# Early score tiles over three buffers, held gates two quads at a time, one-hot rows from GpSimd and ScalarE

## What is computed

```python
def peer_ffn(h, w_q, sub_keys, expert_u, expert_v):     # 8 heads, 128 x 128 experts, top 16
    q = (hb @ w_q).reshape(n, PEER_HEADS, 2, PEER_HALF_2)
    s = jnp.einsum('nhcd,hckd->nhck', q, sub_keys)
    sc, ix = lax.top_k(s, PEER_TOPK)
    cand = sc[:, :, 0, :, None] + sc[:, :, 1, None, :]
    cidx = ix[:, :, 0, :, None] * PEER_N_KEYS + ix[:, :, 1, None, :]
    top, pos = lax.top_k(cand.reshape(n, PEER_HEADS, PEER_TOPK * PEER_TOPK), PEER_TOPK)
    eidx = jnp.take_along_axis(cidx.reshape(n, PEER_HEADS, -1), pos, axis=-1)
    gate = jax.nn.softmax(top, axis=-1)
    act = jax.nn.gelu(jnp.einsum('nhed,nd->nhe', expert_u[eidx], hb), approximate=False)
    return jnp.einsum('nhe,nhed->nd', (gate * act).astype(hb.dtype), expert_v[eidx])
```

## Time and profile before

| | us |
|---|---|
| runs | 4035.78, 4033.04, 4031.42 (median 4033.04) |
| profiled execution | 4032.07, span on the core 4030.0, mean granted TensorE clock 0.918 |

### The profile page before, as it was taken

One profiled execution on the slowest core, in us unless ns is written; L12 is line 12 of the kernel. 1 busy time (PEld: TensorE's weight loads), 2 busy tenths in 40 slices (PEclk: granted clock), 3 DMA queues, 4 the chain that ended last, 5 costly groups with the idle time before them and its releaser, 6 DMA issues. The chain is left out here.

```text
span 4030.0 us, 59683 instructions
## 1 busy us (share of the span) xinstructions
PE 3481.5 (86%) x20736; PEld 3011.1 (75%) x20736; DVE 2486.0 (62%) x5005; ACT 1510.8 (37%) x2312; POOL 427.0 (11%) x460
## 2 busy tenths in 40 slices
PE   6878999999756879999999549797678799999996
PEld 5767899999744767999999537574447679999994
DVE  4688666666545797666666463433326886666664
ACT  4246444444332255444444211111322464444443
POOL 0165000000000373000000000000002640000000
PEclk8999999999878999999999757677789999999998
DMA  4312555555330413555555200000224125555552
GB/s 183 152 53 69 185 186 186 187 187 187 131 128 23 160 32 105 188 187 187 187 187 183 104 0 1 1 1 31 79 89 157 48 76 189 186 186 187 187 187 97
DMA packets 126707, 511.75 MB, mean 127 GB/s; under 512 B 14704, under 2 KB 15344, under 8 KB 119152
## 3 DMA queue, kind: packets, MB, share of 16 engines
q1 hardware_dynamic: 126576, 510.07, 35.3%
HBM read 508.96 MB, written 1.05 MB: 127 GB/s over the span
## 5 line engine op out<-in xcount | busy, mean ns | idle before, releaser
L406 PE MATMUL ps<-xh,uhigh 128*128 128x256 f32 x3072 | 870.3, 283 | 14.5 <-POOL ulow L788 14.5
L408 PE MATMUL ps<-xh,ulow 128*128 128x256 f32 x3072 | 869.2, 283 | 0.0
L407 PE MATMUL ps<-xl,uhigh 128*128 128x256 f32 x3072 | 869.1, 283 | 0.0
L406 PEld LDWEIGHTS ps<-xh,uhigh 128*128 128x128 f32 x3072 | 588.1, 191 | 32.4 <-POOL ulow L788 19.4
L407 PEld LDWEIGHTS ps<-xl,uhigh 128*128 128x128 f32 x3072 | 588.2, 191 | 13.0
L408 PEld LDWEIGHTS ps<-xh,ulow 128*128 128x128 f32 x3072 | 588.1, 191 | 0.0
L753 DVE TENSOR_TENSOR ulow<-stream,uhigh 128x1024 fp32r<-128x1024 f32 x330 | 404.4, 1226 | 201.2 <-ACT uhigh L531 201.0
L531 ACT CAST uhigh<-stream 128x1024 fp32r<-128x1024 f32 x336 | 352.8, 1050 | 436.1 <-DMA stream<-in_u 436.1
L424 PE MATMUL ps<-vhigh,chigh 128*128 128x512 f32 x1536 | 480.0, 394 | 4.6 <-DVE vlow L769 4.2
L424 PE MATMUL ps<-vlow,chigh 128*128 128x512 f32 x1536 | 476.0, 391 | 0.0
L424 PE MATMUL ps<-vhigh,clow 128*128 128x512 f32 x1536 | 474.4, 390 | 0.0
(11 more groups left out here) (425 smaller groups left out, 4670.3 us busy)
## 6 DMA issues: line engine op xcount, KB each, us to landing
stream<-in_u SPq DMA_DIRECT2D x384, 512.0 KB, 4.2
stream<-in_v SPq DMA_DIRECT2D x369, 512.0 KB, 3.5
big<-in_wq SPq DMA_DIRECT2D x24, 1152.0 KB, 7.6
stream<-in_ab_w_in SPq DMA_DIRECT2D x4, 2048.0 KB, 11.1
stream<-in_c_w_qf SPq DMA_DIRECT2D x16, 512.0 KB, 3.5
stream<-in_c_w_ig SPq DMA_DIRECT2D x4, 2048.0 KB, 8.1
stream<-in_w_gates SPq DMA_DIRECT2D x4, 2048.0 KB, 8.1
spare<-in_v SPq DMA_DIRECT2D x15, 512.0 KB, 3.5
```

The lines of the kernel that those rows point to most:

```text
L406: pe.matmul(out, uh[:, b, cols], c.xh[:, k, :], start=k == 0, stop=False)
L407: pe.matmul(out, uh[:, b, cols], c.xl[:, k, :], start=False, stop=False)
L408: ins = pe.matmul(out, ul[:, b, cols], c.xh[:, k, :], start=False, stop=k == KD - 1)
```

## The change

Early tiles rotate over three buffers: a third raw slot (`c.spare`, prefetched with the other two), and third high and low parts in the part of the ring where the `v` slots lie. SyncE therefore loads the first held `v` tiles only once tile 14 has been used. On TensorE tiles 0 to 3 stay behind heads 2 and 3, tiles 4 and 5 come behind heads 4 and 5, and tiles 6 to 15 behind the residual products, after heads 6 and 7. GpSimd's order becomes low parts 0 to 4, `pick(0)`, 5, 6, `pick(1)`, 7, 8, `pick(2)`, then the rest.

The two chosen index tables are cast to fp32r by ScalarE once the last round is stored, and turned by fp32r products with an fp32r identity. The Exp of the weights stands behind that cast in ScalarE's list.

In the gates, B of even quads comes from GpSimd and of odd quads from ScalarE. ScalarE makes the rows of quad g+1 at even g, before it evicts g. `gate_held` handles two quads in one instruction.

```diff
-    MAKER = "DPAPAPAP"
-    made = lambda g: sum(MAKER[x % 8] == MAKER[g % 8] for x in range(g + 1))
+    AFTER = {1: range(0, 4), 2: range(4, 6)}
...
+    early_u = [u[:, 0], u[:, 1], c.spare]
+    early_uh, early_ul = ([x[:, 0], x[:, 1], y] for x, y in ((uh, c.uh_third), (ul, c.ul_third)))
...
             def early(n):
-                sp.wait_ge(early_ul, n - 1)
-                sp.dma_start(u[:, n % 2], u_dram[n]).then_inc(early_landed[n % 2], 16)
-
-            early(2)
+                sp.wait_ge(low_done, n - 2)
+                sp.dma_start(early_u[n % 3], u_dram[n]).then_inc(early_landed[n % 3], 16)
+
+            query(SLOTS)
             early(3)
+            early(4)
+            early(5)
+            for h in range(SLOTS + 1, HEADS):
+                query(h)
+            for n in range(6, HELD):
+                early(n)
+            for b in range(2):
+                sp.wait_ge(low_done, HELD - 2 * b)
+                sp.dma_start(u[:, b], u_dram[HELD + b]).then_inc(u_landed[b], 16)
+            sp.wait_ge(early_used, HELD - 1)
             for n in range(3):
                 sp.dma_start(held_v[n], v_dram[n]).then_inc(held_v_landed[n], 16)
...
-                for n in range(4 * r - 4, 4 * r):
+                for n in AFTER.get(r, ()):
                     early_scores(n)
...
-            for n in range(HELD - 4, HELD):
+            for n in range(6, HELD):
                 early_scores(n)
...
+                    turn = c.ps[:, 4 + s // 2, (s % 2) * T + tt * P:(s % 2) * T + (tt + 1) * P]
+                    if s < 2:
+                        ins = pe.matmul(turn, c.chosen[:, s, tt * P:(tt + 1) * P], c.ident_r, start=True, stop=True)
+                    else:
+                        ins = pe.transpose(turn, c.sel[:, s, tt, :], c.ident[:])
...
-                if MAKER[g % 8] == "A":
-                    pe.wait_ge(act_b_ready, made(g))
-                elif MAKER[g % 8] == "P":
-                    pe.wait_ge(b_ready, made(g))
+                pe.wait_ge(act_b_ready if g % 2 else b_ready, g // 2 + 1)
                 if g < 4:
                     if b >= 2:
                         pe.wait_ge(early_gelu, HELD - 3 + b)
                 else:
-                    pe.wait_ge(dve_moved, g - 3)
+                    pe.wait_ge(dve_moved, g // 2 - 1)
...
-            pe.wait_ge(dve_moved, QUADS - 2)
+            pe.wait_ge(dve_moved, QUADS // 2)
             scores(0, 0, False)
...
+            act.wait_ge(keys_ready, 1)
+            act.copy(c.chosen.rearrange("p s n -> p (s n)"), c.sel[:, 0:2].rearrange("p s t n -> p (s t n)")
+                     ).then_inc(chosen_ready, 1)
             act.wait_ge(shift_ready, ROUNDS)
             act.activation(c.sel[:, 2], c.sel[:, 2], ACT.Exp).then_inc(exp_ready, 1)
...
             for g in range(QUADS):
-                if MAKER[(g + 2) % 8] == "A" and g + 2 < QUADS:
-                    act_keys(g + 2)
+                if g % 2 == 0:
+                    act_keys(g + 1)
                 act.wait_ge(g_ready, g + 1)
...
-            def gate_held(g):
-                dve.wait_ge(act_moved, g + 1)
-                part = held[:, :, 4 * g:4 * g + 4].rearrange("p j t -> p t j")
...
+            def gate_held(x):
+                dve.wait_ge(act_moved, 2 * x + 2)
+                part = held[:, :, 8 * x:8 * x + 8].rearrange("p j t -> p t j")
+                two = c.ps[:, 4 + 2 * (x % 2):6 + 2 * (x % 2), :].rearrange("p b (q j) -> p (b q) j", q=4)
+                dve.tensor_tensor(part, part, two[:, :, 0:HELD], ALU.mult).then_inc(dve_moved, 1)
 
             for g in range(QUADS):
                 if g >= 4:
                     dve.wait_ge(g_ready, g - 3)
-                if MAKER[g % 8] == "D":
-                    dve.tensor_tensor(B[:, g % 4], bc(c.iota, 1, 4), bc(c.selt[:, 1, 4 * g:4 * g + 4], 2, P), ALU.is_equal)
...
-                if g >= 2:
-                    gate_held(g - 2)
-            gate_held(QUADS - 2)
-            gate_held(QUADS - 1)
+                if g % 2 and g >= 3:
+                    gate_held((g - 3) // 2)
+            gate_held(QUADS // 2 - 1)
...
-            early_low(0)
-            early_low(1)
-            for r in range(ROUNDS - 1):
-                early_low(4 * r + 2)
-                early_low(4 * r + 3)
-                pick(r)
-                early_low(4 * r + 4)
-                early_low(4 * r + 5)
-            for n in range(HELD - 2, HELD + 2):
+            for n in range(5):
+                early_low(n)
+            pick(0)
+            early_low(5)
+            early_low(6)
+            pick(1)
+            early_low(7)
+            early_low(8)
+            pick(2)
+            for n in range(9, HELD + 2):
                 early_low(n)
             alone(selt_ready, 1)
             for g in range(QUADS):
-                if MAKER[g % 8] != "P":
+                if g % 2:
                     continue
```

More of the change, by code:

```diff
@@ L250, in select_loads @@
     return {**{b: [(W[:, b], wq_dram[b])] for b in range(SLOTS)},
-            **{FIRST_U + b: [(u[:, b], u_dram[b])] for b in range(2)}}
+            **{FIRST_U + b: [((u[:, 0], u[:, 1], c.spare)[b], u_dram[b])] for b in range(3)}}
 def peer(c, name, wq_dram, u_dram, v_dram, residual, after):
@@ L272, in peer @@
         sem(n) for n in ("eq", "picked", "passed", "passed2", "shift", "exp", "chain"))
-    early_landed = [sem(f"early_landed{b}") for b in range(2)]
-    early_uh, early_ul, early_used, early_gelu = (sem("early_" + n) for n in ("uh", "ul", "used", "gelu"))
-    keys_ready, turned, res_done = sem("keys"), sem("turned"), sem("res")
+    early_landed = [sem(f"early_landed{b}") for b in range(3)]
+    high_done, low_done, early_used, early_gelu = (sem("early_" + n) for n in ("uh", "ul", "used", "gelu"))
+    keys_ready, chosen_ready, turned, res_done = sem("keys"), sem("chosen"), sem("turned"), sem("res")
     a_ready, b_ready, act_b_ready, selt_ready, distances, g_ready, act_moved, dve_moved = (
@@ L475, in scores @@
                     pe.wait_ge(gelu_ready, 2 * i + b - 1)
[L476 removed]
+                score_tile(c.ps[:, 4 + b, 0:T], uh[:, b], ul[:, b]).then_inc(u_used, 1)
             def outputs(i, b):
@@ L535, in early_act @@
                 act.activation(held[:, n, :], early_bank(n), ACT.Gelu).then_inc(early_gelu, 1)
-                if n + 2 < HELD:
-                    early_high(n + 2)
-                else:
-                    u_high(0, n + 2 - HELD, False)
+                if n + 3 < HELD:
+                    early_high(n + 3)
+                elif n + 3 == HELD:
+                    u_high(0, 1, False)
+                elif n + 1 == HELD:
+                    u_high(0, 0, False)
             act.copy(c.xh, c.xt).then_inc(xh_ready, 1)
-            early_high(0)
-            early_high(1)
+            for n in range(3):
+                early_high(n)
+            act.copy(c.ident_r, c.ident).then_inc(xh_ready, 1)
             for h in range(2):
@@ L782, in early_low @@
             def early_low(n):
-                done = early_ul if n < HELD else u_split
                 if n < HELD:
-                    alone(early_uh, n + 1)
-                else:
-                    alone(uh_ready, n - HELD + 1)
-                pool.tensor_tensor(ul[:, n % 2], u[:, n % 2], uh[:, n % 2].bitcast(F32), ALU.subtract).then_inc(done, 1)
+                    alone(high_done, n + 1)
+                    high, low, raw, done = early_uh[n % 3], early_ul[n % 3], early_u[n % 3], low_done
+                else:
+                    alone(uh_ready, 2)
+                    high, low, raw, done = uh[:, n - HELD], ul[:, n - HELD], u[:, n - HELD], u_split
+                pool.tensor_tensor(low, raw, high.bitcast(F32), ALU.subtract).then_inc(done, 1)
             def pick(r):
@@ L2218, in allocate @@
     c.sem = c.sems.open
-    c.first_landed = [nc.alloc_semaphore(name=f"first_landed{b}", num=c.sems.first + 2 * SEMS + b) for b in range(FIRST_U + 2)]
-    c.first_count = [0] * (FIRST_U + 2)
+    c.first_landed = [nc.alloc_semaphore(name=f"first_landed{b}", num=c.sems.first + 2 * SEMS + b) for b in range(FIRST_U + 3)]
+    c.first_count = [0] * (FIRST_U + 3)
     c.ahead = {}
@@ L2262, in allocate @@
     c.uh, c.ul = halves("uhigh", 6 * D, D), halves("ulow", 8 * D, D)
+    c.chosen = halves("chosen", 12 * D, T)
+    c.uh_third, c.ul_third = (nc.alloc_sbuf_tensor_at(n, [P, D], F32R, offset=at + 4 * col)[:]
+                              for n, col in (("uhigh3", 10 * D), ("ulow3", 11 * D)))
+    c.ident_r = ctx.enter_context(nc.sbuf_tensor("ident_r", [P, P], F32R))[:]
     c.ch, c.cl = halves("chigh", 12 * D, T), halves("clow", 12 * D + 2 * T, T)
```

46 lines of the change are left out of this document (19 added, 27 removed).

## The result

The changed kernel takes 4101.53 us (median of four, 4100.16 to 4108.94) against 4033.32 us before: a ratio of 1.0173, 95% interval 1.0155 to 1.0190, slower. The profiled execution took 4101.67 us, 69.6 us more than the one before; its span is 4099.9 instead of 4030.0.

What follows compares the result with a forecast made beforehand. VectorE, delayed by GpSimd, was taken to bound the selection, and no engine alone the gates. Per stage -11.9 + 29.7 + 0.9 = +18.7 us, three stages +56.1, on 4033.04 gives 4089 us; range 4055 to 4118.

Steps and rivals of the forecast that it cites:

- ScalarE's loop, 3.71 us a pair: Gates: ScalarE's rows, TensorE's product and eviction stand in one loop, 3.71 us a pair instead of 2.85.
- Selection, -11.9 a stage: Selection: waits for GpSimd's multiplies and some holds of VectorE go, so it ends 11.9 us earlier a stage.
- Holds in the last round: Last selection round: GpSimd's tiles hold four short VectorE operations, together 6.9 us instead of 8.6 before.
- Exp behind the cast, +2.37 a stage: After the selection: VectorE waits for the Exp behind the index cast, pushing its chain back 2.37 us.
- part 1: Selection with three buffers and ten of sixteen tiles behind the last key product: 11.9 us less a stage.
- SyncE's queue: Load order: every query load still goes before it is needed; early loads wait only for GpSimd's earlier tiles.
- part 2: Chosen indices as fp32r with the Exp behind them: 2.37 us later a stage, the fp32r products saving nothing.
- First score tile, +0.9 a stage: End of the gates: TensorE's first score tile waits for the last gate, 2.9 us to output instead of 2.04.
- The rest of the program, 0: Outside the expert stages: no term in the sum; the loop over 112 other key rows is untouched.
- GpSimd's pace: Rival, gates: ScalarE isn't held by its own rows, pairs go at 2.78 us, 4005 us in all; chance 0.09.
- The cooling of TensorE: Rival, gates: TensorE's clock drops to 1.2 GHz, 28 us a stage, 4173 us in all; chance 0.08.

Runs made afterwards that it cites:

- e1_rows_ahead: The changed kernel with ScalarE making the rows of quad g+3 at even g, not of quad g+1: 4006.03 us, ratio 0.9927.
- e3_gates_only: The kernel before with only the new gates: rows of odd quads on ScalarE at distance one, two quads in a gate: 4123.13 us, ratio 1.0221.
- e10_mended_queue: e4_mended with SyncE issuing the load of tile 17 ahead of that of tile 16: 3996.53 us, ratio 0.9910.
- e11_queue_only: The changed kernel with only SyncE's order edited, the load of tile 17 ahead of that of tile 16: 4101.31 us, ratio 1.0164.
- e4_mended: The changed kernel with rows of quad g+3, Exp ahead of the index cast, first score tile waiting for all gates but the last: 4005.19 us, ratio 0.9928.
- e9_two_more_ahead: The changed kernel with tiles 4 to 7, not 4 and 5, ahead of the last key products: 4102.31 us, ratio 1.0166.
- e5_late_rows: The kernel before with ScalarE making the rows of its quad g at step g instead of g-2: 4235.61 us, ratio 1.0497.
- e14_tile_17_first: e13_three_makers with GpSimd making the low part of tile 17 first, once its high part exists, and tile 16 last: 4002.94 us, ratio 0.9921.
- e13_three_makers: e10_mended_queue with the rows of one quad in eight made by VectorE again: 3994.23 us, ratio 0.9899.

## Why the prediction was right, and where its terms were off

Forecast 4089, range 4055 to 4118, slower; measured 4101.5. The profiled span grew by 69.9 us, the sum said 56.1. The terms below missed by 4.2, 3.8, 1.8, 1.7 and 2.3 us, all in the same direction, so that the forecast was not saved by errors that cancel.

- *ScalarE's loop, 3.71 us a pair.* Measured 3.735; index copy to held cast 123.98 us against 123.4 from the sum (127.0 - 3.63), 1.8 us in three stages. The idle step of 0.85 us and the full clock are as written. GpSimd has more slack than written, 1.39 us idle of each 3.74 and not a quarter: with nothing beside it its four rows take 2.35 us and not the 2.69 of the full stretch before. It is off the path, so that the sum does not feel it. `e1_rows_ahead` shows it by undoing it, `e3_gates_only` by doing it alone.
- *Selection, -11.9 a stage.* Measured -9.4, -10.2, -11.9: 4.2 us less in the sum. All of it is the first query products: they take 9.43 and 9.35 us instead of 7.14 in the first two stages, since in the first, for example, the granted clock was full only from 141.1 on, 4.6 us after they had begun, where in the kernel before it was full 1.3 us before. Take that off and the three are -11.7, -12.4 and -11.7. In the same way round 3 began at 222.77, 4.2 us earlier than before and not 6, and 6.5 with the late clock taken off. It isn't the change's doing: `e10_mended_queue` has the same code up to there and 7.14 us in both stages, `e1_rows_ahead` one of each. A term for it was missing, and it is 2.3 us of chance in each of the first two stages; in the third these products took 8.8 to 9.1 us in every profile.
- *Holds in the last round.* There are four, together 7.5 us above their free times (2.31 - 0.21, 1.74 - 0.21, 2.01 - 0.21, 2.28 - 0.20); the prediction had four of together 6.9. The cast of L670 is one of them: 1.74 instead of 0.21, ending with GpSimd's tile (238.14 + 2.40). For this the prediction had only the Trainium skill ("SBUF — State Buffer", "SBUF: two separate sides": a two-port mode takes the lock too); the trace agrees, with the 1.74 us.
- *Exp behind the cast, +2.37 a stage.* Measured +3.44, +3.84 and +3.63, 3.8 us too small in the sum. The step that failed is in part 1: "SyncE's queue: every query load still goes before it is needed". I looked at the query loads and not at the last two `u` loads, whose order is reversed on ScalarE. The step of part 2 itself was right, as `e11_queue_only` shows (3.55 us against 3.63), but in the changed kernel it hid a second bound: taking it away alone gave 0.03 to 0.26 us a stage (`e4_mended`).
- *First score tile, +0.9 a stage.* 0.95, 0.96 and 2.45. The mechanism is right; in the third stage that tile ran partly at the low clock. TensorE's timeline and the clock there, the answer to the earlier trace rows:

```profile
3346.15 0.52 PE L410 MATMUL ps<-xh,uhigh 128*128 128x256 f32 x1 [1.05 <-DVE big L736]
...
3350.62 0.63 PE L428 MATMUL ps<-vhigh,chigh 128*128 128x512 f32 x2
...
3346.00:3352.00 6.00, 5.85 (x30) 5.60 (x31) 3.72 (x7) 1.57 (x2) 0.00 (x0) 0.72 0.40 105
```

  The same happened in all three stages of `e3_gates_only` (4.33 to 4.48), in two of `e11_queue_only` (5.3) and in two of `e9_two_more_ahead` (5.31 and 4.49), and never where the gates ran at 2.8 us a pair. Of the kernels with rows ahead only `e1_rows_ahead` keeps the wait for the last gate: TensorE idles the same 1.05 us before the score tile there, 84 us after the clock rose in the first stage, and the clock stays. So the wait alone does not bring the fall. The clock of the third stage of the changed kernel shows when it fell:

```profile
3230.20:3346.20 116.00, 62.34 (x493) 57.15 (x492) 80.71 (x273) 88.77 (x217) 67.97 (x117) 1.00 0.00 1
3346.20:3349.70 3.50, 3.50 (x17) 3.50 (x18) 3.43 (x6) 1.37 (x2) 0.00 (x0) 0.51 0.12 21
```

  In each of the eight stages in which it fell, it had been full for 116 us, the fall coming between 0.9 us before the start of the score tile and 0.2 us behind it; in the other four stages of these kernels TensorE was at least 0.9 us into its score tile 116 us after the rise, and the clock stayed. Why the fall came just then, these runs don't show.
- *The rest of the program, 0.* 2.3 us more; over the profiles here it was 0 to 7 us longer than before, and the cause stays open.

Of the rivals, GpSimd's pace did not hold because of the program order, and did as soon as the order was mended: `e1_rows_ahead` gives 4006 us, near the 4005 of that rival, with ScalarE (2.78 us), not GpSimd, as the one that sets the pace. The cooling of TensorE, priced at 28 us a stage, did not come in the gates of the changed kernel, where its idle step is 1.7 us, and came in `e5_late_rows`, where it is 2.6.

## What to carry to other kernels

Where an engine both makes an operand and takes away the product, count how many items lie between the two in its program: at distance one the whole latency of the other engine stands in its loop, whatever the busy sums promise. An order of loads that doesn't match the order in which they are needed costs nothing until what follows becomes the late one; so after a gain, look at the last items of each queue again. And a wait that can be removed may cover another of nearly the same length, so that removing one alone shows nothing.

## What the runs showed of the hardware that I had not expected

- The granted clock of the same products behind the same idle stretch rises some 5 us earlier or later from run to run: 32 query products take 7.1 or 9.4 us, in the same kernel in different stages. It moves each of the first two stages by 2.3 us, together a tenth of a percent of the time, without any change of code.
- With 2.0 us of products in 3.7 us and idle steps of 1.7 us the clock stayed at 1.00 from 275 to 325 in the changed kernel; with idle steps of 2.6 us it was 0.71 in the mean (`e5_late_rows`). At the end of the slower gates it fell in 8 of the 12 stages of the changed kernel, `e3_gates_only`, `e11_queue_only` and `e9_two_more_ahead`, and in none of the three of `e1_rows_ahead`, whose gates take 31 us less.
- Beside a GpSimd that works 2.40 us of each 2.88, four operations of VectorE that take 0.2 us when free were held in one round, for up to 2.3 us. One operation of GpSimd that started some 6 us earlier cost the kernel 9 us (`e14_tile_17_first` against `e13_three_makers`), as it met other work of VectorE.
